# Expert weights with eight neighbouring rows on a partition, and VectorE block transposes of the activations, in a one-core two-model kernel

## The reference, cut to what matters

```
def ec_moe(h, w_router, w_gate, w_up, w_down):
    cap = max(1, EC_FACTOR * n // N_EXPERTS)                    # 32
    aff = jax.nn.softmax(jnp.einsum('bnd,de->bne', h, w_router).astype(jnp.float32), axis=-1)
    gate, idx = lax.top_k(jnp.swapaxes(aff, 1, 2), cap)
    xs = jax.vmap(lambda hb, ib: hb[ib])(h, idx)
    a = jax.nn.silu(jnp.einsum('becd,edf->becf', xs, w_gate)) * jnp.einsum('becd,edf->becf', xs, w_up)
    out = jnp.einsum('becf,efd->becd', a, w_down) * gate[..., None].astype(h.dtype)
    return (scatter-add of out over idx)
```

## Time and profile before

| | |
|---|---|
| time, median of 3 runs | 2891.28 us (2888.82 to 2893.14) |
| the profiled execution | 2901.17 us |
| its span | 2899.3 us |
| granted TensorE clock, mean | 0.888 |
| PE busy | 2229.3 us (77%) |
| PE weight loads busy | 1565.7 us (54%) |
| DVE busy | 951.8 us (33%) |
| ACT busy | 753.5 us (26%) |
| bytes moved by DMA | 679.32 MB, mean 234 GB/s |

### The profile page before, as it was taken

How to read it: one execution, slowest core, us unless ns; L and a number is a source line. 1 busy time by engine, 2 the same in 40 slices (tenths; PEclk the granted TensorE clock), 3 DMA queues, 4 the chain that set the end, 5 groups by cost and what they waited for, 6 DMA issues and landing times.

```text
span 2899.3 us, 36128 instructions
## 1 busy us (share of the span) xinstructions
PE 2229.3 (77%) x16228; PEld 1565.7 (54%) x16228; DVE 951.8 (33%) x1461; ACT 753.5 (26%) x1124; POOL 85.6 (3%) x117
## 2 busy tenths in 40 slices
PE   5977886565566766566566997657699999999999
PEld 3743443222222442222224986636499898886897
DVE  3544443000000240000004433564554544444543
ACT  3322111000000110000004434421354444445542
POOL 0000000000000000000000100000011010000010
PEclk8977787888888879889878998878799999999999
DMA  7266427999999629999996543301255555553552
GB/s 261 74 223 212 172 99 289 409 409 409 409 409 409 248 86 409 409 409 409 409 409 236 175 174 118 131 1 60 66 166 182 169 189 186 185 175 134 168 182 104
DMA packets 272090, 679.32 MB, mean 234 GB/s; under 512 B 9696, under 2 KB 103264, under 8 KB 271680
## 3 DMA queue, kind: packets, MB, share of 16 engines
q1 hardware_dynamic: 265472, 664.49, 61.1%
q10 hardware_dynamic: 4992, 6.62, 0.7%
q0 software_dynamic: 1472, 5.90, 0.6%
HBM read 675.94 MB, written 1.05 MB: 233 GB/s over the span
## 4 chain that ended last, share of the span: by engine, by line
PE 58%; DMA 28%; DVE 8%; ACT 4%; issue 2%; SPq 0%; DVEq 0%; ACTq 0%
PE ps L253 39%; DMA ring<-in_w_exp_gate 24%; PE ps L1631 3%; PE ps L1662 3%; PE ps L730 2%; PE ps L2206 2%; DMA ring<-in_w_exp_down 2%; DMA ring<-in_even_w_in 1%; DVE ring_r L649 1%; PE ps L582 1%; PE ps L738 1%; PE ps L591 1%; PE ps L592 1%; PE ps L595 1%; ACT seam_SQ L472 1%
## 5 line engine op out<-in xcount | busy, mean ns | idle before, releaser
L253 PE MATMUL ps<-HH,ring_r 128*128 128x256 f32 x2720 | 535.6, 282 | 14.6 <-ACT dif_QT L2631 6.9
L1631 PE MATMUL ps<-ring,XS 128*32 128x256 f32 x4096 | 297.1, 440 | 208.8 <-DMA ring<-in_w_exp_gate 129.3
L253 PEld LDWEIGHTS ps<-HH,ring_r 128*128 128x128 f32 x2720 | 437.1, 190 | 15.3 <-ACT dif_QT L2631 7.1
L649 DVE TENSOR_TENSOR ring_r<-ring,ring_r 128x2048 fp32r<-128x2048 f32 (+2 forms) x152 | 324.6, 2177 | 258.1 <-ACT ring_r L640 258.1
L1631 PEld LDWEIGHTS ps<-ring,XS 128*32 128x32 f32 x4096 | 136.4, 123 | 399.9 <-DMA ring<-in_w_exp_gate 190.5
L253 PE MATMUL ps<-HL,ring_r 128*128 128x256 f32 x1136 | 320.5, 282 | 0.0
L640 ACT ACTIVATE ring_r<-ring 128x2048 fp32r<-128x2048 f32 (+2 forms) x152 | 268.7, 1818 | 194.5 <-PE ps L253 110.1
L1649 PE MATMUL ps<-ring,AT 128*32 128x512 f32 x1024 | 179.3, 837 | 137.2 <-DMA ring<-in_w_exp_down 136.0
L253 PEld LDWEIGHTS ps<-HL,ring_r 128*128 128x128 f32 x1136 | 216.0, 190 | 0.2
L1722 DVE TENSOR_TENSOR AA<-SG,ps 128x256 f32<-128x256 f32 x32 | 13.5, 421 | 584.6 <-PE ps L1631 584.6
L253 PE MATMUL ps<-ring_r,AH 128*128 128x512 f32 x576 | 191.6, 396 | 0.0
(11 more groups left out here) (493 smaller groups left out, 2990.8 us busy)
## 6 DMA issues: line engine op xcount, KB each, us to landing
ring<-in_w_exp_gate SPq DMA_DIRECT2D x64, 2048.0 KB, 24.0
ring<-in_w_exp_up SPq DMA_DIRECT2D x64, 2048.0 KB, 24.1
ring<-in_w_exp_down SPq DMA_DIRECT2D x64, 2048.0 KB, 24.1
ring<-in_ffn_wgu SPq DMA_DIRECT2D x88, 1024.0 KB, 7.7
ring<-in_w_mod SPq DMA_DIRECT2D x24, 2048.0 KB, 7.9
ring<-in_ffn_wd SPq DMA_DIRECT2D x20, 2048.0 KB, 7.8
ring<-in_odd_w_in SPq DMA_DIRECT2D x12, 2048.0 KB, 8.0
ring<-in_even_w_in SPq DMA_DIRECT2D x6, 2048.0 KB, 7.8
```

The source lines that it names most:

```text
L253: ins = e.matmul(out, l, r, start=start and i == 0, stop=stop and i == n - 1, skip_group_check=True)
L649: v.tensor_tensor(lo[:, c], s[:, c], hi[:, c].bitcast(F32), ALU.subtract).then_inc(*E.up("split_dve", name, q))
L1631: ins = e.matmul(self.GU[which][32 * j:32 * j + 32, :], self.XS[:, 4 * hk + k, 32 * n:32 * n + 32], W[:, k, 256 * j:256 * j + 256], start= ...
```

## The change

It has four parts.

- `sp_neighbours` takes the place of `sp_rows` for the experts' matrices. Row `8 p + k` of the matrix now goes to partition p; a half (four neighbouring rows, k0 to k0 + 3) is one piece of 16 KB in memory, and pieces of neighbouring partitions lie 32 KB apart.
- The other operand must follow. `every8` picks columns k, 8 + k, 16 + k, ... of a row. The transposes before the router and the gathering matmuls read their stationary operand with that step (32 bytes between elements); the router's weights are loaded in the same order.
- Shift, scale and g of the experts' input must be in that order too. For blocks 6 to 9 of each layer the row is turned by eight matmuls of 64 columns in place of four of 128, and the bias comes from new tiles `g2` and `b2`, which GpSimd loads at its very start by 18 small DMAs (single elements, and runs of 8). VectorE waits for them before it adds the first such bias.
- With units `8 p + k` on partition p, `AT` needs only transposes within blocks of 32 by 32. One VectorE transpose of `AA` (read with a step of 8 elements) writes `AT`. TensorE's two transposes, `TR` and VectorE's copy go.

```
+def every8(a, k):
+    return a.rearrange("p (q k) -> p k q", k=8)[:, k, :]
+def sp_neighbours(S, sp, w, ids, name, W, k0):
+    s, before, sem = S.R.take(ids, name)
+    w.wait_ge(S.E.at("used", before) if before else None)
+    sp.dma_start(s.rearrange("p (k n) -> p k n", k=4), W.rearrange("(p k) n -> p k n", k=8)[:, k0:k0 + 4, :]).then_inc(*S.E.up(sem, by=16))
+    S.E.alias(sem, "loaded", name)
...
-            a.dma_start(S.router[i], S.I["w_router"][i].rearrange("(k p) e -> p k e", p=128)).then_inc(*E.up("routers", by=16))
+            a.dma_start(S.router[i], S.I["w_router"][i].rearrange("(p k) e -> p k e", k=8)).then_inc(*E.up("routers", by=16))
...
+    def pool(self, g, w):
+        for i in range(2):
+            for k in range(8):
+                c = at + 8 * i + k
+                g.dma_start(S.g2[16 * k:16 * k + 16, i, :], S.I["vc"][:, c:c + 1].rearrange("(a b) c -> a (b c)", b=8),
+                            allow_slow_non_contiguous=True).then_inc(*E.up("second", by=16))
+            g.dma_start(S.b2[:, i, :, :], S.I["b_mod"][i:i + 1, 3072:5120].rearrange("a (w p k) -> (a p) w k", w=2, k=8)).then_inc(*E.up("second", by=16))
...
-        for q in range(4):
-            ins = e.matmul(ps[:, 2 * q:2 * q + 2], row[:, 128 * q:128 * q + 128], S.pick, start=True, stop=True, skip_group_check=True)
+        if blk in self.SECOND:
+            h = HALF[blk % 2]
+            for k in range(8):
+                ins = e.matmul(ps[h, 2 * k:2 * k + 2], every8(row, k), S.pick, start=True, stop=True, skip_group_check=True)
...
-            mm(e, ps, [(x[:, t, c], self.PN[:, t, :]) for t in range(2) for x in (self.XH, self.XL)]).then_inc(*E.up("moe_pe", "xs", i, k))
+            mm(e, ps, [(every8(x[:, t, :], k), self.PN[:, t, :]) for t in range(2) for x in (self.XH, self.XL)]).then_inc(*E.up("moe_pe", "xs", i, k))
...
-            w.wait_ge(E.at("moe_dve", "act", i, n), E.at("moe_dve", "at", i, n - 1) if n else None)
-            for hh in range(2):
-                ins = e.transpose(self.TR[:, 128 * hh:128 * hh + 128], self.AA[:, 128 * hh:128 * hh + 128], S.ident)
-            ins.then_inc(*E.up("moe_pe", "turned", i, n))
...
-            w.wait_ge(E.at("moe_pe", "turned", i, n))
-            v.tensor_copy(self.AT.rearrange("p a b c -> p (a b c)"), self.TR).then_inc(*E.up("moe_dve", "at", i, n))
+            w.wait_ge(E.at("moe_dve", "act", i, n), E.at("moe_pe", "down", i, n - 1, 1) if n else None)
+            v.transpose(self.AT, self.AA.rearrange("p (c k) -> p k c", k=8)).then_inc(*E.up("moe_dve", "at", i, n))
```

More of the change, by code:

```diff
@@ L326, in __init__ @@
         self.pick = M.take("pick", 8)[:, 0:2]
+        self.g2, self.b2 = M.take("g2", 2, 8), M.take("b2", 2, 2, 8)
         self.after_first = M.top
@@ L358, in dve_rms, with pe_columns @@
         v.tensor_scalar(out, src, st[:, 1:2], None, ALU.mult).then_inc(*E.up(sem, "normed", *key))
-    def pe_columns(self, e, w, sem, key, rows, nk, ids, evac, *ready, first=0):
+    def pe_columns(self, e, w, sem, key, rows, nk, ids, evac, *ready, first=0, of=lambda a, k: a[:, k * 128:(k + 1) * 128]):
         E = self.E
@@ L369, in pe_columns @@
                     ins = e.transpose(ps[:, (2 * u + tt) * 128:(2 * u + tt + 1) * 128],
-                                      rows[tt][:, (kc + u) * 128:(kc + u + 1) * 128], self.ident)
+                                      of(rows[tt], kc + u), self.ident)
             ins.then_inc(*E.up(sem, "col", *key, kc))
@@ L711 @@
 class Modulation:
+    SECOND = (6, 7, 8, 9)
     def __init__(self, S):
@@ L736, in pe_block @@
         w.wait_ge(E.at("mod_dve", "row", n), E.at("mod_dve", "pick"))
-        for q in range(4):
-            ins = e.matmul(ps[:, 2 * q:2 * q + 2], row[:, 128 * q:128 * q + 128], S.pick, start=True, stop=True, skip_group_check=True)
+        if blk in self.SECOND:
+            h = HALF[blk % 2]
+            for k in range(8):
+                ins = e.matmul(ps[h, 2 * k:2 * k + 2], every8(row, k), S.pick, start=True, stop=True, skip_group_check=True)
+        else:
+            for q in range(4):
+                ins = e.matmul(ps[:, 2 * q:2 * q + 2], row[:, 128 * q:128 * q + 128], S.pick, start=True, stop=True, skip_group_check=True)
         ins.then_inc(*E.up("mod_pe", "turned", n))
@@ L749, in dve_block @@
         w.wait_ge(E.at("mod_pe", "turned", n))
+        if blk in self.SECOND:
+            h, which = HALF[blk % 2], blk // 2 - 3
+            w.wait_ge(*E.end("second"))
+            v.tensor_tensor(S.colm[i][h, 24 + 8 * which:32 + 8 * which, :], ps[h, 0:16].rearrange("p (k t) -> p k t", k=8),
+                            S.b2[h, i, which, :].unsqueeze(2).broadcast_to([64, 8, 2]), ALU.add).then_inc(*E.up("mod_dve", "column", n))
+            yield
+            return
         v.tensor_tensor(S.colm[i][:, 4 * blk:4 * blk + 4, :], ps[:, 0:8].rearrange("p (q t) -> p q t", q=4),
@@ L756, in dve_scale @@
         c = S.colm[i]
-        g = S.col("g1" if which == 0 else "g2", 8, 8 * i).unsqueeze(2).broadcast_to([128, 8, 2])
+        g = (S.col("g1", 8, 8 * i) if which == 0 else S.g2[:, i, :]).unsqueeze(2).broadcast_to([128, 8, 2])
         w.wait_ge(E.last("mod_dve"))
@@ L1557, in __init__ @@
         self.SG, self.AA = M.take("SG", 256), M.take("AA", 256)
-        self.AT = M.take("AT", 2, 4, 32)
+        self.AT = M.take("AT", 8, 32)
         self.OS = M.take("OS", D)
@@ L1584, in sp @@
                     w.wait_ge(*E.end(*LANES, *ATT), E.at("even_dve", "hsum", 1))
-                sp_rows(S, sp, w, self.SLOTS, (name, i, n, hk), S.I[name][i, n], 4 * hk, 4)
+                sp_neighbours(S, sp, w, self.SLOTS, (name, i, n, hk), S.I[name][i, n], 4 * hk)
             for hk in range(2):
-                sp_rows(S, sp, w, self.SLOTS, ("w_exp_down", i, n, hk), S.I["w_exp_down"][i, n], 4 * hk, 4)
+                sp_neighbours(S, sp, w, self.SLOTS, ("w_exp_down", i, n, hk), S.I["w_exp_down"][i, n], 4 * hk)
     def before(self, i):
@@ L1597, in pe @@
         S.pe_columns(e, w, "moe_pe", ("h", i), halves(self.XN), 8, six, ("moe_dve", "moe_act"),
-                     *(E.at("moe_dve", "normed", "h", i, t) for t in range(2)))
+                     *(E.at("moe_dve", "normed", "h", i, t) for t in range(2)), of=every8)
         lg, free = B.take(six, ("logits", i), ("moe_act", "exp", i))
@@ L1648, in pe @@
                         kk = 4 * hk + j
-                        ins = e.matmul(self.O[hf][32 * j:32 * j + 32, :], self.AT[:, kk % 2, kk // 2, :], W[:, j, 512 * hf:512 * hf + 512],
+                        ins = e.matmul(self.O[hf][32 * j:32 * j + 32, :], self.AT[:, kk, :], W[:, j, 512 * hf:512 * hf + 512],
                                        start=hk == 0, stop=hk == 1, skip_group_check=True)
@@ L3095, in gpsimd @@
         S, E, w = self.S, self.S.E, Waits(g)
+        self.start.pool(g, w)
         self.even.pool(g, w)
```

4 lines of the change are left out of this document (2 added, 2 removed).

## The result

| | before | after |
|---|---|---|
| time, median of 4 runs each | 2892.1 us | 2858.7 us (2848.18 to 2863.8) |
| the profiled execution | 2901.17 us | 2863.8 us |
| its span | 2899.3 us | 2861.9 us |
| granted TensorE clock, mean | 0.888 | 0.879 |

The ratio is 0.9878, 95% interval [0.9853, 0.9902]: 33 us less, between 28 and 43. The forecast was 2857.

What follows compares the result with a forecast made beforehand. The expert stages were taken to be bound by DMA rate, 180 loads on the path. Loads -38.9, turn 0, strided operands +2, modulation +3, start 0 sum to -33.9 us: 2891.3 becomes 2857 us, 8 in 10 range 2843 to 2898.

Steps and rivals of the forecast that it cites:

- The bound: Both expert stages run at the DMA engines' pace, 409 GB/s, with TensorE waiting; 180 loads are on the path.
- The loads: Experts' 2 MB loads: 16 KB packets at 612 ns, 0.216 us less a load, times 180: -38.9 us (-33 to -50).
- The turn: Activations turned within an expert by one VectorE transpose of 0.42 to 1.64 us, hidden: 0.
- the cover named: The down load: `AT` is ready at 785.4, but the product waits until 787.1 for its load.
- Strided stationary operands: Weight loads with a 32-byte step before each expert stage: +2 us, on the transposes, within 0 and 12.8.
- Modulation: Eight blocks in the attention stage, eight matmuls of 64 columns for four of 128: +3 us, within 0 and +12.
- 0.4 x 8: Modulation: 0.4 us extra for each of eight blocks, most but not all on the chain, making +3 us.
- The start: Wait for `ctx` behind the router's small packets: 1.6 us saved on each engine, GpSimd's small loads cost 2.0; net 0, within 2.
- The sum: Whole kernel: -38.9 + 0 + 2 + 3 + 0 = -33.9 us, median 2857 us.
- Rival 1: Experts' loads: packets stay at 4 KB or the rate has another lid at 409 GB/s; 2896 us; chance 0.14.
- Rival 2: Experts' loads: 16 KB pieces 32 KB apart are read more slowly, up to +460 us, 3350 us; chance 0.11.

Runs made afterwards that it cites:

- loads alone: Kernel before with only the experts' loads in the new order (16 KB runs), products pairing wrong rows: 2849.33 us, ratio 0.9834.
- four DMAs: Changed kernel with each 2 MB load issued as four DMAs in runs of 4 KB, same places: 2897.42 us, ratio 0.9997 to the kernel before.
- modulation as before: Changed kernel with blocks 6 to 9 of each layer turned by four matmuls of 128 columns again: 2851.97 us, ratio 0.984 to the kernel before.
- two rows at a time: Changed kernel with blocks 6 and 7, and 8 and 9, turned together by eight matmuls of 128 columns: 2853.86 us, ratio 0.9839 to the kernel before.
- changed kernel once more: The changed kernel unaltered, measured again against the kernel before (2898.2 us) on one chip: 2856.27 us, ratio 0.9859.
- turn alone: Kernel before with only VectorE's block transpose in place of TensorE's two transposes and the copy: 2895.45 us, ratio 0.9997.
- router's loads alone: Kernel before with only the router's weights loaded in the new order, 256 runs of 512 bytes for 2048 of 64: 2890.38 us, ratio 0.9971.
- last: Kernel before with its small-packet router loads moved to the end of ScalarE's first DMAs, behind `ctx` and the constants: 2897.48 us, ratio 1.0001.
- from GpSimd: Kernel before (2898.22 us) with its router loads issued by GpSimd in place of ScalarE, layout unchanged: 2888.51 us, ratio 0.9967.
- two DMAs: Changed kernel with each half of a matrix loaded by two DMAs in runs of 8 KB: 2869.09 us, ratio 0.9905 to the kernel before.

## Why the prediction was right, and where it was not

**The bound, right.** The stages went at the pace of the DMA engines, TensorE kept waiting, and the 180 loads on the path were the whole of the stages' gain.

**The loads, right in mechanism, and in size by some luck.** 612 ns a packet was taken between bounds of 606 and 618; 614 was measured. -38.9 us was forecast, -39.4 measured. The two sizes, 4 and 8 KB, were enough to see a fixed price; its size was seen too large (11.5 ns from a stretch of 1.5 us, 9 in truth) and the middle between this and no further gain took half of it back. The two errors cancelled: that part is luck.

**The turn, right:** 0. The transpose takes 0.64 us, inside the bounds 0.42 and 1.64, under the cover named.

**Strided stationary operands, right in sum and wrong in place.** The view by tile, after:

```profile
L376 PEld LDWEIGHTS ps<-base,moe_XN x32: 186/226/226, 434.0 to 1009.5; 128*128 128x128 f32 x32
L253 PEld LDWEIGHTS ps<-PN,XH x32: 313/333/337, 458.0 to 1042.1; 128*128 128x128 f32 x32
```

The extra was laid on the transposes; these cost nothing (226 ns, 230 before). The loads of `XH` and `XL` rose from 188 to 333 ns. In layer 0 that is hidden behind the matmuls almost wholly: the 32 of them are 9.58 us in the chain, 9.35 before; in layer 1, 10.63 against 9.73. About 1 us in all, 2 forecast.

What the step costs depends on the clock in these rows. From 457.5 to 459.5 us of the kernel before, granted clock 0.50, a load of neighbouring columns of `XH` takes 330 ns, and with the step (after, 458 to 460 us, 0.50) it takes 333: no price. A few us later, at 1.00, they take 188 and 332. All 32 transposes run at 0.50 to 0.52, before and after, so that they cost nothing may be the clock's doing and not theirs; no run has them with the step at the upper level. There is something to lose there: where `ret_G` is transposed in the kernel before, at 1.00, a load of neighbouring columns takes 141 ns. The rule of the Trainium skill (SBUF — State Buffer, Door 1: The DMA port swizzle), that an access whose elements lie on new 16-byte lines pays, agrees with the 332 ns against 188 at the upper level; at the lower no price shows (333 against 330). What it costs the kernel, cover decides.

**Modulation, the mis-sized term.** +3 was forecast within bounds of 0 and 12; 6.5 to 8 us came up to the first expert load, of which some 2 were given back by the router's product at a higher clock. The step that failed is "0.4 x 8": it took a price near the lower end between half the columns in half the time and twice the instructions. The rows show that one load of 64 columns 32 bytes apart (217 ns) is no shorter than one of 128 neighbouring ones at the upper clock (192), and the chain that nearly all of it is on the path.

**The start, the step that failed.** "Net 0, within 2" became -6.7. The packets were priced by their own busy time, less than a third of the ACT queue's share. Their real price is the turn that each gives to the other queue. The counts of both queues in a short window would have shown it before: they are equal. The share that GpSimd's small loads were to cost in return didn't appear in the start (50.1 us with them, 49.6 without).

**The sum.** By the stretches of the table: loads -39.4, start -6.7, up to the first expert load +9.1, from there to the seventh load -1.7 (router's product -1.9, gathering +0.2), between the layers +1.4 (gathering +0.9 of it), the rest -0.1, together -37.4. The medians differ by 33.4, and -33.9 was forecast, nearer than its parts deserved: the errors of start and modulation have opposite signs, and that they cancel is luck.

**The rivals fell.** Rival 1 (no gain beyond 4 KB, a lid at 409 GB/s): 428 and even 431 GB/s. The preferred limit of 4096 bytes that the Trainium skill gives for a packet (DMA: Bandwidth & Descriptors, SWDGE vs HWDGE vs iDMA), taken as a rule for these loads, would have meant 409; packets of 8, 16 and 32 KB are seen here, each cheaper by the byte. Rival 2 (16 KB pieces slow): 614 ns, below the 637 from which it decided. The instruction fetches at 0.96 us say nothing of loads into the ring.

**What stays open.** Stretches of identical code differ between profiles. Between the layers (last down product of layer 0 to the seventh load of layer 1) the length goes with the granted TensorE clock:

| kernels | us | granted clock |
|---|---|---|
| loads alone, four DMAs, modulation as before, two rows at a time | 119.0 to 119.2 | 0.82 to 0.83 |
| changed kernel once more | 121.0 | 0.81 |
| before, turn alone, router's loads alone, last, from GpSimd | 121.9 to 123.0 | 0.79 to 0.80 |
| changed kernel, two DMAs | 124.3 to 124.4 | 0.76 |

What sets the clock there was not tested. The rest after layer 1 took 1355.7 to 1361.9 us at 0.94 in all of them; TensorE is busy for 1196 us in the shortest and 1203 in the longest with the same 8884 instructions, so the difference is in how long its instructions last. These differences are as large as the small terms; why the first comparison gave 33 us and the second 42 isn't separated further. Most of it is on the side of the kernel before: 2892.1 us in the 4 runs of the first, 2896.8 to 2898.2 in the 9 to 25 runs of each later group, while the changed kernel took 2858.7 and 2856.3.

## What to carry to other kernels

Where a stage runs at the rate of its loads, count packets and divide: a fixed price for each packet, read from two sizes over a long window, tells what longer runs will give, and a layout that lets a partition take neighbouring rows collects it. Price small packets by the turns they cost the queue beside them, and by the time their issuing holds an engine, not by their own busy share. What a new layout demands elsewhere (strided weights, rows turned in eighths) is paid where no load hides it: look there for the share that will be given back.

## What the runs showed of the hardware

- A DMA packet of the hardware queue costs 9 ns + 37.8 ns for each KB on one engine, from 4 to 32 KB; by that line 16 engines would end at 433 GB/s, an estimate (302.7 ns for 8 KB). The number of DMAs (one, two or four for 2 MB) made no difference.
- Two hardware queues shared the engines one packet for one packet, 677 against 674 in 4 us, at 2 KB and 64 bytes.
- Two loads of 1024 pieces of 64 bytes held the issuing engine for 9.46 us right behind eight other loads (2.44 us as its third and fourth load, in the kernel before); GpSimd issued the same two in 1.95 us, as packets of 2 KB.
- A float32 transpose of 128 x 256 in blocks of 32 on VectorE, read with a step of 8 elements, takes 634 ns.
- Weight loads for matmuls, 128 columns 32 bytes apart: 332 to 335 ns at a granted clock of 1.00 and of 0.50; neighbouring columns 188 to 192 ns at 1.00, 330 to 333 at 0.50. 64 columns with the step: 217 ns at both. For transposes at 0.50 to 0.52: 226 ns with the step, 230 without.
- The same 32 instructions of a product with 16 columns took 7.0 us at a granted clock of 0.50 and 5.1 us at 0.71.
